# Statistics of the first normalization inside the output projection of a two-layer hybrid block, with other edits at the start, in a readout loop and at the end

## What is computed

```
sh1, sc1, g1, sh2, sc2, g2 = split(silu(c) @ ada_w[layer] + ada_b[layer], 6)      # for context tokens from c_ctx
y = token_mixers(x * (1 + sc1) + sh1, ...)          # attention, DeltaNet, retention, latent attention, concatenated
x = layer_norm(ALPHA * x + g1 * (y @ w_out), ln1_g, ln1_b)
x = layer_norm(ALPHA * x + g2 * (square(relu((x * (1 + sc2) + sh2) @ w_ff1)) @ w_ff2), ln2_g, ln2_b)
# layer_norm: (x - mean) * rsqrt(mean((x - mean)**2) + 1e-5) * g + b, over the 1024 channels of a token
# retention, out: o = inner + cross; (o - mean) * rsqrt(var) per head, times silu(gate)
```

## Time and profile before

| | us |
|---|---|
| timed runs, median of 3 | 4561.45 |
| lowest and highest | 4555.86, 4567.37 |
| profiled execution | 4553.73 |
| its span | 4551.9 |
| TensorE busy (matmul) | 4057.3 |
| VectorE busy | 2026.1 |
| ScalarE busy | 1161.5 |
| POOL busy | 956.7 |

### The profile page before, as it was taken

How to read it: one execution, slowest core, us unless ns; L and a number is a source line. 1 busy time by engine, 2 the same in 40 slices (tenths; PEclk the granted TensorE clock), 3 DMA queues, 4 the chain that set the end, 5 groups by cost and what they waited for, 6 DMA issues and landing times. The chain is left out here.

```text
span 4551.9 us, 77693 instructions
## 1 busy us (share of the span) xinstructions
PE 4057.3 (89%) x33172; PEld 3310.8 (73%) x33172; DVE 2026.1 (45%) x3628; ACT 1161.5 (26%) x2531; POOL 956.7 (21%) x679
## 2 busy tenths in 40 slices
PE   4999988869979999999995999789599798999996
PEld 3655876758866888888874657688488676888884
DVE  3344446644443433333335354466444435443443
ACT  2344214223331211111114443132233412110111
POOL 0000100022202433333310000100132114444440
PEclk8988989979989999999997999899699899999998
DMA  3221000100000011111111110000100010111111
GB/s 159 81 105 56 20 29 1 69 2 3 3 29 28 28 38 38 45 37 37 37 37 45 75 75 29 19 20 19 42 3 3 21 37 28 47 54 47 46 46 46
DMA packets 23303, 180.21 MB, mean 40 GB/s; under 512 B 2416, under 2 KB 2672, under 8 KB 7536
## 3 DMA queue, kind: packets, MB, share of 16 engines
q1 hardware_dynamic: 21296, 166.73, 10.0%
q10 hardware_dynamic: 1728, 9.40, 0.5%
HBM read 167.73 MB, written 8.39 MB: 39 GB/s over the span
## 5 line engine op out<-in xcount | busy, mean ns | idle before, releaser
L1130 PE MATMUL ps<-Yn_parts,ring_parts 128*128 128x512 f32 (+1 forms) x3840 | 797.8, 369 | 9.6 <-issue 7.8
L1130 PEld LDWEIGHTS ps<-Yn_parts,ring_parts 128*128 128x128 f32 x3840 | 670.4, 189 | 134.7 <-issue 8.6
L1130 PE MATMUL ps<-temp_parts,ring_parts 128*128 128x512 f32 (+1 forms) x2560 | 727.2, 370 | 17.4 <-DVE Hn_parts L2179 17.4
L643 PE MATMUL ps<-ring_parts,Xn_parts 128*128 128x256 f32 x2560 | 508.6, 294 | 58.5 <-DVE ring_parts L1742 52.7
L2130 DVE SCALAR_TENSOR_TENSOR Xn<-ps,mods,Xn 128x256 f32<-128x256 f32 (+1 forms) x360 | 250.9, 697 | 694.8 <-PE ps L1130 545.3
L2383 POOL TENSOR_TENSOR ring_parts<-ring,consts 128x2048 fp32r<-128x2048 f32 x64 | 296.0, 4625 | 1193.4 <-DMA ring<-in_ff 1193.4
L1130 PEld LDWEIGHTS ps<-temp_parts,ring_parts 128*128 128x128 f32 x2560 | 466.3, 189 | 100.2 <-DVE Hn_parts L2179 18.9
L1130 PE MATMUL ps<-Hn_parts,ring_parts 128*128 128x512 f32 (+1 forms) x1280 | 472.3, 369 | 0.0
L643 PEld LDWEIGHTS ps<-ring_parts,Xn_parts 128*128 128x128 f32 x2560 | 421.3, 197 | 62.4 <-issue 53.6
L1616 ACT ACTIVATE Yn<-ps 128x256 f32<-128x256 f32 (+1 forms) x160 | 88.6, 554 | 1255.8 <-PE ps L1130 1255.8
L662 PE MATMUL ps<-consts,temp 128*128 128x128 f32 (+1 forms) x1416 | 259.7, 302 | 127.0 <-DVE temp L1989 54.1
(11 more groups left out here) (292 smaller groups left out, 6038.4 us busy)
## 6 DMA issues: line engine op xcount, KB each, us to landing
ring<-in_ff SPq DMA_DIRECT2D x64, 1024.0 KB, 4.8
ring<-in_ada SPq DMA_DIRECT2D x24, 2048.0 KB, 8.4
ring<-in_halves SPq DMA_DIRECT2D x30, 1024.0 KB, 4.8
Xn<-in_x ACTq DMA_DIRECT2D x1, 5120.0 KB, 26.8
Xn<-in_x SPq DMA_DIRECT2D x1, 5120.0 KB, 15.9
kept_x<-Xn SPq DMA_DIRECT2D x2, 2048.0 KB, 8.0
Xn<-kept_x SPq DMA_DIRECT2D x1, 4096.0 KB, 14.0
out_x<-Xn SPq DMA_DIRECT2D x1, 4096.0 KB, 11.7
```

What stands on the lines that cost most here:

```text
L643: m = pe.matmul(ps[:, bank, 0:256], (G_hi, H_lo)[a][:, k, t * P:(t + 1) * P], w[b][:, k, :], start=(k == 0 and part == 0), stop=(k == KT - ...
L1130: m = pe.matmul(ps[:, bank, 0:hi - lo], w[a][:, k, j * P:(j + 1) * P], x[b][:, k, lo:hi], start=(k == 0 and part == 0), stop=(k == k_n - 1 ...
```

## The change

- **Order of the output projection.** Halves 0 and 1 as before; then halves 2 and 3 segment by segment (`out_order`), so that a segment's X is complete four to eight products before the projection ends. The fourth half has a place of its own in Hn (`last_raw`, `last_hi`, `last_lo`) and is loaded early; so are the first MLP halves (`ready_first`), and POOL splits the one of them during the projection.
- **Mean.** VectorE adds up the eight blocks as it evacuates them (`sum_step`), in a place in Hn, for the last segment partly in PSUM bank 7; one matmul with ones spreads the sum.
- **Variance.** The squares are the stationary operand, 128 tokens at a time, and two columns of ones move through: tokens come to lie on partitions, two columns each. Root and reciprocal work on these; VectorE multiplies the identity by the result (`diag_of`) and one matmul with ones returns it across the partitions (`rstd_of`).
- **Placing.** These three steps of segment c-1 stand between matmuls of products of segment c (`hooks`), those of the last segment in the MLP's first group, which takes the earlier segments first with one weight half, then with the other (`first_order`). The barrier after the projection is gone.
- **Retention readout.** Turning goes to bank 3 and behind the product with the values, which now waits for `r_o`; VectorE weighs the scores before it updates the state.
- **Start.** All loads go to SP's queue: small tensors, ada chunks 0 to 3 (2 and 3 into Hn), X.
- **End.** The output leaves in four transfers of 1 MB, each as its four channel blocks of a segment are done; the barrier is not waited for.

The core of the diff:

```diff
+        def chunk_at(n_):
+            if n_ in (2, 3):
+                return Hn[:, (n_ - 2) * KT * CW:(n_ - 1) * KT * CW]
+            return ring[:, n_ % 2, :]
...
+        def out_order(L):
+            segs = range(len(tokens(L)))
+            return [(i, c, j) for i in (0, 1) for c in segs for j in range(2)] + [(i, c, j) for c in segs for i in (2, 3) for j in range(2)]
+        def ready_first(L):
+            return HALF_AT[(PREP_HALVES + OUT_HALVES) * L + PREP_HALVES + 1] % 2
+        def first_order(L):
+            last, e = len(tokens(L)) - 1, ready_first(L)
+            return [(c, s, j) for s in (e, 1 - e) for c in range(last) for j in range(2)] + [(last, s, j) for s in range(2) for j in range(2)]
...
+                if n_ in (4, 5):
+                    sp.wait_ge(sems["chunk_used"], 2)
...
+                if n_ in OUT_LAST:
+                    sp.wait_ge(sems["out_free"], OUT_LAST.index(n_) + 1)
...
+            for to, of in ((cc[:], d["cc"]), (consts[:], d["consts"]), (ada_b[:], d["ada_b"]), (params[:], d["params"][0])):
+                sp.dma_start(to, of).then_inc(sems["consts_in"], 16)
...
+                    if n_ == 3:
+                        sp.dma_start(X[:, :, :], d["x"]).then_inc(sems["x_in"], 16)
...
+                for n_, s in enumerate((ready_first(L), 1 - ready_first(L))):
+                    sp.wait_ge(sems["half_free"], (PREP_HALVES + OUT_HALVES) * (L + 1) - 2 + 2 * n_)
...
+            n_out = 2 * len(SEGMENTS)
+            for lo, hi in SEGMENTS[1:]:
+                for k in (0, 4):
+                    n_out += 1
+                    sp.wait_ge(sems["ln_out"], n_out)
+                    sp.dma_start(d["out"][:, k:k + 4, lo - NCTX:hi - NCTX], X[:, k:k + 4, lo:hi]).then_inc(sems["out_done"], 16)
+            sp.wait_ge(sems["out_done"], 64)
...
-                    if s_ >= 2:
-                        pe.wait_ge(sems["normed"], nth("normed", s_ - 1))
-                        pe.wait_ge(sems["r_o"], nth("r_o", s_ - 1))
-                        for j in range(2):
-                            m = turn(ps[:, 2, j * P:(j + 1) * P], r_oc[:, s_ % 2, j * P:(j + 1) * P])
-                        m.then_inc(sems["yT_mm"], tally("yT_mm"))
...
                         pe.wait_ge(sems["r_state"], nth("r_state", NT + s_ - 1))
+                        if s_ >= 3:
+                            pe.wait_ge(sems["yT_sb"], nth("yT_sb", s_ - 2))
...
-                            pe.wait_ge(sems["yT_sb"], nth("yT_sb", n_))
+                            pe.wait_ge(sems["r_o"], nth("r_o", n_))
...
+                    if s_ >= 2:
+                        pe.wait_ge(sems["normed"], nth("normed", s_ - 1))
+                        pe.wait_ge(sems["r_state"], nth("r_state", NT + min(s_, NT - 1)))
+                        if s_ > NT:
+                            pe.wait_ge(sems["yT_sb"], nth("yT_sb", s_ - 2))
+                        for j in range(2):
+                            m = turn(ps[:, 3, j * P:(j + 1) * P], r_oc[:, s_ % 2, j * P:(j + 1) * P])
+                        m.then_inc(sems["yT_mm"], tally("yT_mm"))
...
+            def mean_of(c, bank, of, w_):
+                pe.wait_ge(sems["ln_sum"], nth("ln_sum", c + 1))
+                pe.matmul(ps[:, bank, 0:w_], ones, of, start=True, stop=True).then_inc(sems["ln_mean"], tally("ln_mean"))
+            def var_of(c, bank, of, lo, hi):
+                pe.wait_ge(sems["ln_centred"], nth("ln_centred", 2 * c + 2))
+                for k in range(KT):
+                    if k % 4 == 0:
+                        pe.wait_ge(sems["ln_square"], nth("ln_square", 2 * c + k // 4 + 1))
+                    for n_ in range((hi - lo) // P):
+                        m = pe.matmul(ps[:, bank, 2 * n_:2 * n_ + 2], of[:, k, lo + n_ * P:lo + (n_ + 1) * P], ones[:, 0:2],
+                                      start=(k == 0 and n_ == 0), stop=(k == KT - 1), skip_group_check=True)
+                m.then_inc(sems["ln_var"], tally("ln_var"))
+            def rstd_of(c, bank, diag, w_):
+                pe.wait_ge(sems["ln_diag"], nth("ln_diag", c + 1))
+                pe.matmul(ps[:, bank, 0:w_], ones, diag, start=True, stop=True).then_inc(sems["ln_rstd"], tally("ln_rstd"))
...
+                cols = tokens(L)
+                short = cols[0][1] - cols[0][0] == 256
+                hooks = {}
+                for c in range(1, len(cols)):
+                    wide = cols[c - 1][1] - cols[c - 1][0] == 512
+                    hooks[(2, c, 0)] = {3: lambda c=c: settle_mean(L, c - 1)}
+                    hooks[(3, c, 0) if wide else (2, c, 1)] = {2: lambda c=c: settle_var(L, c - 1)}
+                    hooks[(3, c, 1) if wide else (3, c, 0)] = {2: lambda c=c: settle_rstd(L, c - 1)}
+                halves_ = {}
+                for n_, (i, c, j) in enumerate(out_order(L)):
+                    if i not in halves_:
+                        halves_[i] = next_half()
+                    if i == 0 and j == 0:
+                        pe.wait_ge(sems["h_split"], nth("h_split", c + 1))
+                    if n_ >= 4:
+                        pe.wait_ge(sems["evac_dve"], nth("evac_dve", n_ - 3))
+                    channel_product(n_ % 4, halves_[i], j, (H_hi, Y_lo), *cols[c], hooks.get((i, c, j), {}))
...
+                order, last = first_order(L), len(cols) - 1
+                hooks = {2 if last == 2 else 1: {2: lambda: settle_var(L, last)}, 3 if last == 2 else 2: {2: lambda: settle_rstd(L, last)}}
+                if last == 2:
+                    hooks[0] = {3: lambda: settle_mean(L, last)}
+                else:
+                    settle_mean(L, last)
+                for n_, (c, s, j) in enumerate(order):
                     pe.wait_ge(sems["h_split"], nth("h_split", c + 1))
...
+                    pe.wait_ge(sems["split"], nth("split", 1 if s == ready_first(L) else 2))
+                    if n_ >= 4:
+                        pe.wait_ge(sems["relu"], nth("relu", n_ - 3))
+                    else:
+                        pe.wait_ge(sems["evac_dve"], nth("evac_dve", n_ - 3))
+                    product(n_ % 4, up_weights(s), j, (H_hi, H_lo), KT, *cols[c], hooks.get(n_, {})).then_inc(sems["prod"], tally("prod"))
...
+            def square_of(c, out, lo, hi):
+                for b in range(2):
+                    ks = slice(4 * b, 4 * b + 4)
+                    act.wait_ge(sems["ln_centred"], nth("ln_centred", 2 * c + b + 1))
+                    A(out[:, ks, lo:hi], X[:, ks, lo:hi], ACT.Square).then_inc(sems["ln_square"], tally("ln_square"))
+            def root_of(c, bank, eps, n_t):
+                act.wait_ge(sems["ln_var"], nth("ln_var", c + 1))
+                A(ln_root[c][:, 0:n_t, :], ps[:, bank, 0:2 * n_t].rearrange("p (t a) -> p t a", a=2), ACT.Sqrt, bias=eps, scale=1.0 / DM)\
+                    .then_inc(sems["ln_root"], tally("ln_root"))
...
+                for c in range(last):
+                    square(c)
+                    root(c)
+                    modulated(c)
+                square(last)
+                first_group(0, last)
+                root(last)
+                first_group(last, last + 1)
+                modulated(last)
+                first_group(last + 1, up)
...
+            def centre_of(c, bank, lo, hi):
+                dve.wait_ge(sems["ln_mean"], nth("ln_mean", c + 1))
+                for b in range(2):
+                    ks = slice(4 * b, 4 * b + 4)
+                    STT(X[:, ks, lo:hi], spread(ps[:, bank, 0:hi - lo], 1, 4), -1.0 / DM, X[:, ks, lo:hi], ALU.mult, ALU.add)\
+                        .then_inc(sems["ln_centred"], tally("ln_centred"))
+            def diag_of(c, out, n_t):
+                dve.wait_ge(sems["ln_root"], nth("ln_root", c + 1))
+                link(dve.reciprocal(ln_inv[c][:, 0:n_t, :], ln_root[c][:, 0:n_t, :]))
+                TT(out.rearrange("p (t a) -> p t a", a=P), spread(ident, 1, n_t), spread(ln_inv[c][:, 0:n_t, 0], 2, P), ALU.mult)\
+                    .then_inc(sems["ln_diag"], tally("ln_diag"))
+            def scale_of(c, bank, lo, hi):
+                dve.wait_ge(sems["ln_rstd"], nth("ln_rstd", c + 1))
+                for b in range(2):
+                    ks = slice(4 * b, 4 * b + 4)
+                    TT(X[:, ks, lo:hi], X[:, ks, lo:hi], spread(ps[:, bank, 0:hi - lo], 1, 4), ALU.mult)\
+                        .then_inc(sems["ln_scaled"], tally("ln_scaled"))
+            def sum_step(j, lo, hi, partial, whole):
+                x_ = X[:, j, lo:hi]
+                if j == 1:
+                    TT(partial, X[:, 0, lo:hi], x_, ALU.add)
+                if 1 < j < KT - 1:
+                    link(TT(partial, partial, x_, ALU.add))
+                if j == KT - 1:
+                    TT(whole, partial, x_, ALU.add).then_inc(sems["ln_sum"], tally("ln_sum"))
...
+            def settle_low(L, c):
+                lo, hi = tokens(L)[c]
+                for b in range(2):
+                    ks = slice(4 * b, 4 * b + 4)
```

(52 more changed lines are left out.)

302 lines of the change are left out of this document (112 added, 190 removed).

## The result

The changed kernel takes 4506.97 us (median of four, 4490.07 to 4520.47), the kernel before 4563.78 beside it; the ratio is 0.9876, 95% interval 0.9832 to 0.992. A second set of six gave 4509.1, ratio 0.9884 (0.9865 to 0.9903). The forecast was 4489 with 4466 to 4513 as its range. That the total is near hides that two of its four terms were far off, in opposite directions. The profile, which was to fall to 4481, missed by 38.

A forecast was written before the change was run, and what follows sets the result against it. TensorE, busy 89% of the span, was taken as the bound. Start 21.0, readout 26, projection with normalization 18.6 and end 7.1 sum to 72.7 us, off the median 4561.45: forecast 4489, range 4466 to 4513.

The forecast's parts named there:

- The rearranged projection and normalization: Output projection to MLP in both layers: statistics moved inside the projection save 7.7 us in layer 1, 10.9 in layer 0.
- 32 matmuls of two columns; sixteen such took 1.95, so 3.9: Variance of a 512-column segment in the rearranged normalization: priced at 3.9 us from a row of the earlier trace.
- clock: 2.0 and 3.2: Projection and first MLP group, both layers: time lost to a lower TensorE clock after pauses, 2.0 and 3.2 us.
- the working's 68.4: Layer 0, two short products and the mean end 68.4 us after T, the first segment's eighth block; then a pause.
- POOL's split: Layer 0's projection: POOL splitting MLP weights holds up VectorE instructions with two SBUF operands, priced at 1.0 us.
- slower: Rival, chance 0.03: TensorE drops to 1.2 GHz in the interrupted projection and through the first up group, +91 us, 4652.
- the settlement only changes its place: Rival, chance 0.12: VectorE's queue and POOL's lock take all the rearranged normalization's saving, 4507 us.
- The readout: Retention readout, both layers: VectorE's waits for TensorE shrink, 26 us saved, bounds 10 and 34.
- I take 8 of 12: Retention readout rounds before the last: 8 of 12 us of VectorE's waits a layer go if TensorE keeps pace.
- the 5.0 of the last round: Last round of the retention readout: its wait goes for certain, 5 us a layer.
- Start and end: Kernel's start: modulation at 39.2 instead of 60.2, 21.0 us saved; end: four early stores, 7.1 us saved.
- even sharing: Rival at the start, chance 0.07: engines serve all transfers evenly, chunks land together, 3 us saved for 21, 4507.

The follow-up runs named there:

- e1: The kernel before with only the start, retention readout and end edits, the output projection and first normalization left as before: 4482.54 us.
- e9: The kernel before run once more, unchanged, for a second profile: 4552.09 us (one run).
- e8: The kernel before with the retention readout edit alone: 4515.74 us.
- The best version: e5 with, in layer 0, the first segment's low parts formed later, after the second's centring and an evacuation of the third: 4458.94 us.
- e5: The changed kernel with the variance's squares and ones in the rounded type and 128 columns of ones in place of 2: 4484.0 us.
- e12: e5 with six small ScalarE copies added as idle ahead of the barrier before layer 1's latent attention: 4472.65 us.

## Why the prediction was right, and where it was wrong

**The rearranged projection and normalization is the step that failed**: 18.6 us saved were forecast, 24.5 were lost (1904.1 for the changed kernel against 1879.6, the mean of the old place's four), 43.1 off. Two terms make it up.
- "32 matmuls of two columns; sixteen such took 1.95, so 3.9" took the x16 of the earlier trace rows for sixteen matmuls of the program. They were eight: an f32 matmul is two instructions in the trace. Thirty-two are 64 rows and 7.3 us. Over five groups that is 34.0 for 17.6: 16.4 us. The old variance cost 7.0 a segment (the line below has layer 1's two; the earlier trace rows has 7.15 for the mean before it), so the main saving claimed for turning the operands round never existed.
- "clock: 2.0 and 3.2" after pauses. The clock also fell in and behind two-column groups without a pause ahead of them, and stayed at half through one that stood behind a pause. Changed kernel against 128 columns (two profiles of each): 25.9 us of stage time.

```profile
3749.16 14.00 PE L1198 MATMUL ps<-Hn,consts 128*128 128x512 f32 x32 [1.36 <-ACT Hn L1589]
```

The two sum to 42.3. The rest of this step came much as worked out: MLP start 18.5 us after layer 1's projection (18.5), the pause in layer 0 11.0 (11.4; the working's 68.4 should be near 67.9, which moves the pause and not the sum), the low parts' wait 4.6 (4.2), the waits for diagonals 1.4 (1.1), 3.7 before the down half (3.9), the last segment's 5.6 (5.3). POOL's split cost 2.3 (1.0): two of VectorE's sum steps, called hidden, stood beside it for 3.47 and 4.06 us, and the first mean of layer 0 waited. With the two terms set right, the edit was worth 2 us; the 128-wide kernel's stages show 1.4, which is inside their spread.

The rival "slower" had part of the mechanism and the wrong size: TensorE did stay at half clock through interrupted work, 30.7 us at a stretch, but not through the 164 us that it needed. It looked for the trigger in the pauses alone. The rival "the settlement only changes its place" has the measured number, 4507, by accident: its causes, VectorE's queue and POOL's lock, cost about what was priced.

**The readout** was the other mis-sized term: 26 forecast, 38.8 measured, above the stated bound of 34. "I take 8 of 12" in the rounds was 13.2, so TensorE keeps pace throughout (7.8 us a round, where the loop without waits was worked out as 7.9); the 5.0 of the last round was 6.2 with the tail's better clock.

**Start and end** were right to 1.5 and 0.6 us. The start's shortfall is mostly X, which was to be there at 38.5 to 39 and landed at 39.7. The half clock of the second pair of chunk products (3.64 each, where the one at 18.11 took 1.93) cost under 1 us more: in e1 (first line) that chain was done at 36.9, and modulation waited for X until 39.95. The old start hung on the clock instead and began modulation at 60.23, 62.02 (e9) and 66.69 (e8, second line), so the edit is worth 19.5 to 26 us.

```profile
39.95 2.35 DVE L1775 TENSOR_SCALAR Hn<-Xn,mods 128x256 f32<-128x256 f32 x7 [3.07 <-DMA Xn<-in_x]
```

```profile
66.69 2.67 DVE L1755 TENSOR_SCALAR Hn<-Xn,mods 128x256 f32<-128x256 f32 x8
```

The Trainium skill, "DMA: Bandwidth & Descriptors", section on queues, rings and completion order, has each DMA engine take the descriptors of one queue in ring order. The trace agrees: the chunks were used in issue order, the first products at 13.28 and 18.11, then 27.80; even sharing is out.

**The sum**: 19.5 + 38.8 + 7.7 - 24.5 = 41.5. The two profiles differ by 35.0, the timed medians by 57 and 50. That remainder, 6.5 us one way and up to 15 the other, is of the size of the clock patterns in the attention stages and the old start, and no run ties it to one cause. Taken off the same median, 41.5 would have given 4520, outside the range: that the time fell inside it is luck, one term's error against another's and a remainder that nobody forecast.

The best version beats both kernels: 4458.94, 48 us under the changed one. Only 41 of that is in the settlement stages (1902.3 to 1861.0), and of its 25 us over e5 only 7 are earned by the edit. Against the kernel that leaves the rearrangement out (e1) its stages are 22 us shorter; the 128-wide kernel, at 4481.65, is level with e1's 4482.54.

## What to carry to other kernels

Before a row prices a new operation, divide its count by what one line of the program issues: an f32 matmul here stood twice. Swap stationary and moving operand only after counting weight loads; and where a thin matmul lasts as long as its weight load anyway, more columns are free: here 128 in place of two gave back 25 us. Judge an edit of 10 us by its stage in the profile, since an unchanged stage moved by 15 us where 1.7 us of idle was added ahead of it.

## What was not expected of the hardware

- In five places 32 two-column matmuls back to back (16 in one), which the trace shows as a TensorE busy throughout, had the granted clock at half in or right behind them; at one of them it was at half already, from the pause ahead. The same count at the same pace with 128 columns had it at full in the other four. What it is in two-column matmuls that lets the clock fall, no run shows. Two windows of the changed kernel's groups, and two of the 128-wide kernel's (same columns as above):

```profile
1403.66:1412.10 8.44, 8.44 (x65) 8.44 (x64) 0.52 (x1) 0.00 (x0) 0.00 (x0) 0.83 0.00 0
...
3686.00:3696.60 10.60, 10.60 (x66) 10.59 (x64) 0.53 (x1) 0.00 (x0) 0.00 (x0) 0.65 0.01 2
```

```profile
1397.34:1404.40 7.06, 7.06 (x65) 7.05 (x64) 0.53 (x1) 0.00 (x0) 0.00 (x0) 1.00 0.00 0
...
3661.90:3669.00 7.10, 7.10 (x66) 7.10 (x64) 0.50 (x1) 0.00 (x0) 0.00 (x0) 1.00 0.01 2
```

- A weight load of 128 f32 or rounded columns and its matmul follow each other every 0.114 us at full clock, and every 0.218 us in the group that ran wholly at half clock (13.94/64). The Trainium skill, "TensorE: Matmul & The Clock Gate", section "LDWEIGHTS (loading the stationary operand)", gives P/1.2 ns for a load of P columns, 107 ns for these 128; the first is near it, the second twice as long.
- Layer 1's latent attention and retention, the same code, took 364.2 to 384.1 us by the clock alone: 372.8 or 372.9 in all five kernels whose first half-clock stretch began 6.3 us in, but 380.9 and 364.2 in two where it began 7.5 and 7.6 us in. The Trainium skill, "TensorE: Matmul & The Clock Gate", Part 1 on the clock gate, says that its rhythm runs free and isn't reset when a kernel starts; what added idle did in e12 fits that, and shows no more.
